# Five matmuls per weight block in place of six in three FFN down projections

## The reference

```
def swiglu_ffn(h, w_gate, w_up, w_down):
    return (jax.nn.silu(h @ w_gate) * (h @ w_up)) @ w_down

x = x + 0.5 * swiglu_ffn(rms_norm(x, norm_ffn_pre[i]), ...)
x = x + mixer(rms_norm(x, norm_mix[i]))
x = x + 0.5 * swiglu_ffn(rms_norm(x, norm_ffn_post[i]), ...)
```

## Time and profile before

| | |
|---|---|
| median of three runs | 2246.74 us (2245.89 to 2248.54) |
| span of the profiled execution | 2247.4 us |
| PE busy | 2145.6 us, 95% of the span |
| weight loads (PEld) busy | 2072.4 us, 92% |
| DVE busy | 1055.8 us, 47% |
| ACT busy | 709.5 us, 32% |
| POOL busy | 269.8 us, 12% |

### The profile page before, as it was taken

The page is one execution under the profiler, slowest core; times in us unless marked ns, Lnnn a source line. Parts: engine busy times, 40 slices in busy tenths (PEclk is TensorE's granted clock), DMA queues, the critical chain, the costliest instruction groups (busy, mean ns, idle before and its releaser), DMA issues.

```text
span 2247.4 us, 39202 instructions
## 1 busy us (share of the span) xinstructions
PE 2145.6 (95%) x16165; PEld 2072.4 (92%) x16165; DVE 1055.8 (47%) x1264; ACT 709.5 (32%) x1063; POOL 269.8 (12%) x214
## 2 busy tenths in 40 slices
PE   8999999887779999999999999999999899999997
PEld 8999999866649999999999999999887699999997
DVE  4444433389985544432344443323446464444322
ACT  5222222354543322222232222222333233222222
POOL 0000002276633000001100000111000030000000
PEclk9999999988889999999999999999899999999999
DMA  4322323211102323233323223233223223223321
GB/s 137 93 84 84 90 84 87 89 57 38 38 23 66 94 87 90 84 87 87 89 85 93 84 85 88 85 89 86 66 66 122 76 81 105 86 84 92 91 83 66
DMA packets 338764, 185.65 MB, mean 83 GB/s; under 512 B 6012, under 2 KB 334942, under 8 KB 338668
## 3 DMA queue, kind: packets, MB, share of 16 engines
q1 hardware_dynamic: 335228, 172.78, 26.4%
q0 software_dynamic: 3200, 11.64, 1.5%
q10 hardware_dynamic: 256, 0.10, 0.0%
HBM read 177.29 MB, written 8.05 MB: 82 GB/s over the span
## 4 chain that ended last, share of the span: by engine, by line
PE 83%; DVE 10%; issue 3%; ACT 2%; DMA 1%; POOL 1%; ACTq 0%; SPq 0%; DVEq 0%; POOLq 0%
PE ps L425 75%; PE ps L446 4%; DVE pool_sum L1419 3%; DVE cv L1419 2%; DVE w_lo L412 1%; ACT w_hi L405 1%; DVE prod L1445 1%; PE ps L1081 1%; PE ps L1087 0%; DMA hist_in<-in_state_conv 0%; PE ps L905 0%; DVE cv L1451 0%; POOL pool_sum L782 0%; PE ps L994 0%; DMA pin<-in_gla_onorm_g 0%
## 5 line engine op out<-in xcount | busy, mean ns | idle before, releaser
L425 PE MATMUL ps<-xg_hi,w_hi 128*128 128x272 f32 x3344 | 702.0, 291 | 3.6 <-DVE tb L1428 1.6
L425 PE MATMUL ps<-xg_hi,w_lo 128*128 128x272 f32 x3344 | 696.7, 290 | 0.0
L425 PE MATMUL ps<-xg_lo,w_hi 128*128 128x272 f32 x3344 | 694.4, 289 | 0.0
L405 ACT ACTIVATE w_hi<-raw 128x1024 fp32r<-128x1024 f32 x329 | 348.0, 1060 | 1021.6 <-PE ps L425 971.6
L412 DVE TENSOR_TENSOR w_lo<-raw,w_hi 128x1024 fp32r<-128x1024 f32 x329 | 424.7, 1293 | 446.6 <-ACT w_hi L405 446.0
L425 PEld LDWEIGHTS ps<-xg_hi,w_hi 128*128 128x128 f32 x3344 | 532.5, 190 | 7.7 <-issue 2.5
L425 PEld LDWEIGHTS ps<-xg_lo,w_hi 128*128 128x128 f32 x3344 | 530.7, 190 | 0.0
L425 PEld LDWEIGHTS ps<-xg_hi,w_lo 128*128 128x128 f32 x3344 | 526.9, 191 | 0.0
L425 PE MATMUL ps<-h_hi,w_hi 128*128 128x272 f32 x1536 | 318.3, 288 | 1.7 <-DVE x L1480 0.9
L425 PE MATMUL ps<-h_hi,w_lo 128*128 128x272 f32 x1536 | 317.9, 288 | 0.0
L425 PE MATMUL ps<-h_lo,w_hi 128*128 128x272 f32 x1536 | 316.7, 288 | 0.0
(11 more groups left out here) (260 smaller groups left out, 1473.5 us busy)
## 6 DMA issues: line engine op xcount, KB each, us to landing
raw<-in_ffn_w_gate SPq DMA_DIRECT2D x88, 512.0 KB, 3.8
raw<-in_ffn_w_up SPq DMA_DIRECT2D x88, 512.0 KB, 3.8
raw<-in_ffn_w_down SPq DMA_DIRECT2D x64, 512.0 KB, 3.7
raw<-in_gla_w_in SPq DMA_DIRECT2D x25, 512.0 KB, 3.8
raw<-in_ffn_w_down SPq DMA_DIRECT2D x32, 384.0 KB, 3.2
raw<-in_conv_w_pw SPq DMA_DIRECT2D x24, 512.0 KB, 3.8
raw<-in_gla_w_out SPq DMA_DIRECT2D x8, 512.0 KB, 3.7
st<-in_state_gla POOLq DMA_DIRECT2D x4, 1024.0 KB, 9.7
```

The source lines that it names most:

```text
L405: nc.scalar.activation(w_hi[:, n % RING], raw[:, n % RAW], ACT.Copy).then_inc(w_high, 1)
L425: last = nc.tensor.matmul(ps[:, 2 * pair + c, 0:HALF], w[:, r, k, :], a[:, k0 + k, c * HALF:(c + 1) * HALF], start=(k0 + k == 0 and w is w ...
```

## The change

In the down stages of f00, f01 and f10, `h_hi` and `h_lo` become one buffer `hl`, in which each block has for each half c its 272 hi columns and behind them its 272 lo columns. One matmul with w_hi then takes the 272 hi columns of half c and the first 92 lo columns (364, into one bank), for c = 0 and 1; a third takes the last 180 lo columns of both halves (2 x 180, into a third bank); w_lo takes the hi columns as before (2 x 272). A unit so occupies three banks, and units alternate between banks 0 to 2 and 4 to 6; PE waits for the unit two back. The two other stages that used `h_hi` and `h_lo` (the second conv projection and the attention's output) keep separate buffers at the same place. f11's down stage reads `hl` and keeps six matmuls of 272.

DVE adds a unit to x in three instructions: the main columns (2 x 272), then, after a wait on that one, the first 92 lo columns of each half (2 x 92), and the last 180 (2 x 180). Only the last counts `evac`. The waits of PE ahead of the stages behind f00, f01 and f10 ask for one unit more.

```diff
-        h_hi = sb("h_hi", [P, F, T], F32R)
-        HLO = taken[0]
-        h_lo = sb("h_lo", [P, F, T], F32R)
+        hl = sb("hl", [P, F, 2, T], F32R)
+        HLO = HHI + F * T * 4
+        h_hi = at("h_hi", [P, M, T], F32R, HHI)
+        h_lo = at("h_lo", [P, M, T], F32R, HLO)
...
+        REST = 180
+        LEAD = HALF - REST
+        def down_main(j):
+            return ps[:, 4 * (j % 2):4 * (j % 2) + 2, 0:HALF]
+        def down_lead(j):
+            return ps[:, 4 * (j % 2):4 * (j % 2) + 2, HALF:HALF + LEAD]
+        def down_rest(j):
+            return ps[:, 4 * (j % 2) + 2, 0:2 * REST].rearrange("p (c n) -> p c n", c=2)
...
+        def down_products(pe, n, j, nk, k0, i, per, ready):
+            pe.wait_ge(w_split, n + 1 + per * i)
+            r = n % RING
+            for k in range(nk):
+                kk = k0 + k
+                if ready is not None:
+                    pe.wait_ge(ready[0], ready[1] + k + 1)
+                for c in range(2):
+                    nc.tensor.matmul(ps[:, 4 * (j % 2) + c, 0:HALF + LEAD], w_hi[:, r, k, :], hl[:, kk, c, 0:HALF + LEAD],
+                                     start=(kk == 0), stop=False)
+                nc.tensor.matmul(down_rest(j), w_hi[:, r, k, :], hl[:, kk, :, HALF + LEAD:T], start=(kk == 0),
+                                 stop=(kk == F - 1))
+                for c in range(2):
+                    last = nc.tensor.matmul(ps[:, 4 * (j % 2) + c, 0:HALF], w_lo[:, r, k, :], hl[:, kk, c, 0:HALF],
+                                            start=False, stop=(kk == F - 1))
+            last.then_inc(w_done, 1)
...
-                pe.wait_ge(evac, u0 - 2)
+                pe.wait_ge(evac, u0 - 1)
...
-                    pe.wait_ge(evac, u0 + j - 3 + 4 * i)
+                    pe.wait_ge(evac, u0 + j - 1 + 4 * i)
                     for c in range(3):
                         k0 = c * SLOT_K
-                        slot_products(pe, s0 + 3 * j + c, (u0 + j) % 4, h_hi, h_lo, nk=min(SLOT_K, F - k0), k0=k0,
-                                      kt=F, i=i, per=12, ready=(h_split, s.h0 + k0) if j == 0 else None)
+                        down_products(pe, s0 + 3 * j + c, j, min(SLOT_K, F - k0), k0, i, 12,
+                                      (h_split, s.h0 + k0) if j == 0 else None)
...
-                    nc.scalar.activation(h_hi[:, 2 * i + p, :], tb[:, p, :], ACT.Copy).then_inc(h_high, 1)
+                    nc.scalar.activation(hl[:, 2 * i + p, :, 0:HALF], halves(tb[:, p, :]), ACT.Copy).then_inc(h_high, 1)
...
-                    nc.vector.tensor_tensor(h_lo[:, 2 * i + p, :], tb[:, p, :], h_hi[:, 2 * i + p, :].bitcast(F32),
-                                            ALU.subtract).then_inc(h_split, 1)
+                    nc.vector.tensor_tensor(hl[:, 2 * i + p, :, HALF:T], halves(tb[:, p, :]),
+                                            hl[:, 2 * i + p, :, 0:HALF].bitcast(F32), ALU.subtract).then_inc(h_split, 1)
...
-                    nc.vector.scalar_tensor_tensor(
-                        out=halves(x[:, m, :]), in0=bank_pair((u0 + j) % 4), scalar=0.5,
-                        in1=halves(x[:, m, :]), op0=ALU.mult, op1=ALU.add).then_inc(evac, 1)
+                    xm = halves(x[:, m, :])
+                    nc.vector.scalar_tensor_tensor(out=xm, in0=down_main(j), scalar=0.5, in1=xm, op0=ALU.mult,
+                                                   op1=ALU.add).then_inc(d_part, 1)
+                    dve.wait_ge(d_part, parted[id(s)] + j + 1 + 4 * i)
+                    nc.vector.scalar_tensor_tensor(out=xm[:, :, 0:LEAD], in0=down_lead(j), scalar=0.5,
+                                                   in1=xm[:, :, 0:LEAD], op0=ALU.mult, op1=ALU.add)
+                    nc.vector.scalar_tensor_tensor(out=xm[:, :, LEAD:HALF], in0=down_rest(j), scalar=0.5,
+                                                   in1=xm[:, :, LEAD:HALF], op0=ALU.mult, op1=ALU.add).then_inc(evac, 1)
                     dve_x_split(dve, s.q + 1, m)
...
-                pe.wait_ge(evac, u0 + j - 3)
+                pe.wait_ge(evac, u0 - 1)
...
-            pe.wait_ge(evac, GN - 3)
+            pe.wait_ge(evac, GN - 1)
```

More of the change, by code:

```diff
@@ L230, in build @@
         s_acc = sem("s_acc")
+        d_part = sem("d_part")
         s_stat = sem("s_stat")
@@ L337, in build @@
         f11 = ffn(1, 1, 5, 5, 7)
+        parted = {id(s): i * M for i, s in enumerate((f00, f01, f10))}
         SLOTS = count["slot"]
@@ L429, in slot_products, with final_products @@
             last.then_inc(w_done, 1)
+        def down_products(pe, n, j, nk, k0, i, per, ready):
[14 more added lines that the diff above has]
+            last.then_inc(w_done, 1)
+        def final_products(pe, n, pair, nk, k0, ready):
+            pe.wait_ge(w_split, n + 1)
+            r = n % RING
+            for k in range(nk):
+                kk = k0 + k
+                if ready is not None:
+                    pe.wait_ge(ready[0], ready[1] + k + 1)
+                for w, a0 in ((w_hi, 0), (w_hi, HALF), (w_lo, 0)):
+                    for c in range(2):
+                        last = nc.tensor.matmul(
+                            ps[:, 2 * pair + c, 0:HALF], w[:, r, k, :], hl[:, kk, c, a0:a0 + HALF],
+                            start=(kk == 0 and w is w_hi and a0 == 0), stop=(kk == F - 1 and w is w_lo))
+            last.then_inc(w_done, 1)
         def wide_products(pe, n, pairs, a_hi, a_lo, ready, high_ready=None):
@@ L1124, in _ @@
                         k0 = c * SLOT_K
-                        slot_products(pe, s0 + 3 * j + c, (u0 + j % 2) % 4, h_hi, h_lo, nk=min(SLOT_K, F - k0), k0=k0,
-                                      kt=F, ready=(h_split, f11.h0 + k0) if j == 0 else None)
+                        final_products(pe, s0 + 3 * j + c, (u0 + j % 2) % 4, min(SLOT_K, F - k0), k0,
+                                       (h_split, f11.h0 + k0) if j == 0 else None)
                 if j:
```

## The result

The changed kernel takes 2261.39 us (median of four runs, 2261.07 to 2261.89), the kernel before 2246.84 in the same comparison: a ratio of 1.0065, 95% interval 1.0051 to 1.0079, 14.6 us slower. That lies above the range of the prediction (2226 to 2250), and the kernel became slower where the forecast (2242.4) had it faster.

What follows compares the result with a forecast made beforehand. PE bounds the kernel, busy 95% of 2247.4 us, the three down stages lasting as long as their matmuls follow each other; 2246.7 - 6.3 (fused matmuls) + 2.0 (later x) = 2242.4 us, range 2226 to 2250.

Steps and rivals of the forecast that it cites:

- part 4: Buffer hl, its two-run writes, the final stage and PE's waits ahead of the next stages: all costed at nothing.
- part 1: Three down stages: one matmul fewer in each of 528 weight blocks, columns unchanged; 6.3 us gained, bounds 1.0 and 22.2.
- three readings: What the 11.95 ns beyond a 272-column matmul's columns hang on: columns, instruction or weight load; gains 1.0, 6.3, 22.2 us.
- the one by columns: Down-stage matmuls: excess grows with columns, only 1.9 ns per instruction; gain 1.0 us, total 2247.7; as a rival, chance 0.28.
- the law per instruction: Down-stage matmuls: each costs width / 2.4 + 11.95 ns; gain 6.3 us, the reading the forecast took, chance 0.45.
- the bounds of 1.0 and 22.2 us: Least and greatest gain for one matmul fewer per block: excess mostly with columns, or weight load hidden behind longer matmuls.
- The weight load as the price: Rival, down stages: the load paces 272 columns and hides behind 364; block 709.7 ns, total 2226.5 us, chance 0.17.
- part 2: Third matmul of each block reads 2 x 180 columns lying 544 apart: taken as nothing, upper bound +31 us.
- the slower rival: Third matmul of each block: the two-run read costs up to 58 ns more; total 2257.7 to 2273 us, chance 0.10.
- part 3: DVE adds x in three instructions, complete 1.0 us later; paid after the first and third stages, +2.0 us (0 to 3.0).

Runs made afterwards that it cites:

- the old wait back: Changed kernel, but ahead of f01's and f11's up stages PE waits for the unit three back again: 2251.01 us against 2246.83 of the kernel before.
- the new wait alone: Kernel before, with only PE's wait ahead of the up stages of f01, f10 and f11 asking one unit more: 2257.91 us against 2246.83.
- the cut 176: Changed kernel with the earlier wait ahead of f01 and f11 and blocks cut 2x368, 2x176, 2x272 in all three stages: 2243.16 us against 2247.08.
- the three additions alone: Kernel before with x added in three instructions (2x272, 2x92, 2x180), the last two with factor 0: 2250.03 us against 2246.83.

## Why the prediction was wrong

**The step that failed most** is in part 4, the edits at nothing: "PE's waits ahead of the next stages ask for one unit more than before, a unit that was finished 16.5 us earlier". That holds where a down stage with units of 16.5 us comes before, as for f10. For f01 and f11 the stage before is a square projection, whose units PE makes 6 us apart, the first four together, and behind which DVE is two units late. The cost was 10.4 to 11.1 us (the old wait back; the new wait alone, whose interval is 8.8 to 14.8), of the measured 14.6. Who waits was read from the code of the down stages only, though the edited line stands in a function that three FFNs share; one look at DVE's additions ahead of f01 in the trace of before would have shown the seventh unit added 4 us after PE was through (725.68 + 0.77 against 722.12). The prediction asked for the cover of each wait, and took one cover for all three.

**The fused matmuls (part 1)**: the term 528 x 11.95 = 6.3 us gained was +0.9 us lost, the 364-column starts 168.3 ns apart and so beyond the 165.3 that was named as the point of failure. Of the three readings the one by columns came nearest (364 at 167.0, no gain), but as a law it fails as well: other cuts gain what the law per instruction says (739.8 against 740.0 and 740.1 measured for 384 and 368), or more. The mistake was to carry one width's excess, 11.95 ns, as a constant to other cuts, when no row had another width; the bounds of 1.0 and 22.2 us, too, did not hold a loss. The weight load as the price is out: no cut comes near 709.7 ns. Part of the miss is the layout, which part 4 put at nothing because "hl has the size of the two buffers that it replaces". Six matmuls of 272 out of hl cost 756.4 ns per block against 751.7 out of two buffers, and against those 756.4 the five matmuls of the change are 3.1 ns cheaper, not 11.95. That the two parts simply add is not shown.

The Trainium skill, "TensorE: Matmul & The Clock Gate", section "Back-to-back issue gap", has 2.5 ns on top of the columns for an isolated matmul at full clock, 154.2 ns for 364 columns (an estimate from the page). The trace disagrees for this type, in a stream with a weight load for each matmul: 168.3 ns at 364 columns, and 125.3 against 115.8 at 272.

**The two-run read (part 2)** cost nothing at this cut, as taken (753.3 ns with one run and with two); the slower rival had the right sign by the wrong mechanism, which is luck. The Trainium skill, "PSUM — Partial Sum Buffer", section "Specifications (TRN2)", says that a non-contiguous access pattern slows matmuls significantly. The runs don't bear that out for a moving operand in two long runs: against one run it was dearer once (753.2 and 746.7 ns), cheaper once (740.1 and 746.7), and equal once.

**The later x (part 3)** was right in place: nothing inside the stages, a price behind f00 and f10 and none behind f01. PE pays it one weight block earlier than forecast, waiting for xg_lo (0.56 us of idle) and not for the sum at L457. The size was 1.0 each and measured 0.81 at the statistics matmuls: the two short additions took 0.35 and 0.52 us where a line through two other widths gave 0.42 and 0.565. In device time it is 1.4 us (with the cut 176) to 3.2 (alone, interval 0.4 to 4.7) against 2.0 expected.

**Not in the sum at all**: f11's down stage, which keeps six matmuls of 272 and only reads hl, went from 137.06 us (2097.46 to 2234.52, the last matmul) to 137.91 (2109.14 to 2247.05), +0.85 us. The rows of before and after:

```profile
2097.46 0.41 PE L425 MATMUL ps<-h_hi,w_hi 128*128 128x272 f32 x2
...
2234.52 0.27 PE L1134 MATMUL ps<-ident,x 128*32 128x128 f32 x1
```

```profile
2109.14 0.66 PE L475 MATMUL ps<-hl,w_hi 128*128 128x272 f32 x4
...
2247.05 0.27 PE L1188 MATMUL ps<-ident,x 128*32 128x128 f32 x1
```

It was costed at nothing because its widths stay. The same 137.9 is seen in every run whose f11 reads hl, and 137.06 in the two whose f11 doesn't (the new wait alone, the three additions alone). It is the layout's price again, 4.8 ns per block.

The sum as measured: the wait 10.4 to 11.1, the additions 1.4 to 3.2, the blocks 0.9, f11 0.85, which is 13.6 to 16.1 for 14.6. What remains open is what sets a block's price by its cut and layout, and so why 180 is dear and 144 is cheap; and whether the three additions cost more than the 1.6 us that the places behind f00 and f10 show. Device times don't settle that: from the end of f00's down stage to the square projection the profiled execution of before took 250.85 us, and that of the new wait alone, whose code is the same there, 253.00.

## What to carry to other kernels

A wait moved by one unit is costed at every place that runs the line, by what the producer has finished at that moment there; an engine that lags by two units behind a burst turned one unit of margin into 4 us of idle PE here, and the clock that fell behind it added a third to a half as much again (2.8 and 4.4 us on 8.0). And a price per matmul that is known at one width only is no constant: with rows of no other width, the honest bounds have both signs, and one run with a cut per stage prices three of them. A new layout of an operand is costed too, also where neither columns nor instructions change.

## What the runs showed of the hardware that was not expected

Blocks of five fp32r matmuls with the same 1632 columns cost from 733.5 to 753.3 ns at the full clock (granted 1.00, 2.4 GHz) by where they are cut, in steps of 3.33 ns. Each of the cuts 180, 176 and 144 cost the same within 0.2 ns in every stage and run that had it, though two matmuls of one width in a block differed by some 10 ns (about 164 and 174 at 368 columns). A matmul of 64 columns was followed by the next start after 29 ns, but the start after that came some 207 ns later, where 124 are usual, so that a block with it cost 826.7 ns. Six matmuls of 272 columns went from 751.7 to 756.4 ns per block when their hi and lo halves came to lie beside each other in one buffer, 0.85 us per 176 blocks. Two idles of about 4 us were each followed by 3 to 6 us at the lower clock: in the profile of the change (0.53 and 0.57 in the windows) that cost 4.4 us on top of the 8.0 of the idles, with the new wait alone (0.75 and 0.62) 2.8 us on the same 8.0.
